# Four places instead of six for first rows, eight instead of six for value rows

## What is computed

```python
def peer_ffn(h, w_q, sub_k1, sub_k2, exp_u, exp_v):       # blocks of 128 tokens
        q1, q2 = jnp.split(split_heads(hb @ w_q, PEER_HEADS), 2, axis=-1)
        ...                                               # top 16 of each half, top 16 of the sums
        idx = jnp.take_along_axis(cand_i, pos, axis=-1)
        gate = jax.nn.softmax(best_s, axis=-1).astype(hb.dtype)
        act = jax.nn.gelu(jnp.einsum('thkd,td->thk', exp_u[idx], hb))
        return jnp.einsum('thk,thkd->td', gate * act, exp_v[idx])
```

## Time and profile before

| | us |
|---|---|
| median of 3 runs | 5725.39 |
| lowest, highest | 5721.04, 5725.57 |
| profiled execution | 5726.25 |
| its span (first to last instruction) | 5724.5 |

### The profile page before, as it was taken

One profiled execution on the slowest core, in us unless ns is written; L12 is line 12 of the kernel. 1 busy time (PEld: TensorE's weight loads), 2 busy tenths in 40 slices (PEclk: granted clock), 3 DMA queues, 4 the chain that ended last, 5 costly groups with the idle time before them and its releaser, 6 DMA issues.

```text
span 5724.5 us, 57220 instructions
## 1 busy us (share of the span) xinstructions
PE 4378.9 (76%) x19168; PEld 2442.8 (43%) x19168; DVE 2919.4 (51%) x7856; ACT 1361.0 (24%) x3807; POOL 2761.2 (48%) x2566
## 2 busy tenths in 40 slices
PE   7988888887987878987855557898777889855555
PEld 4467643433675334653411114567443456511111
DVE  1212756775126767456565541322666654666653
ACT  1411123443212331121211112631143311111111
POOL 0000556666205555666576771000566556677776
PEclk9789888888998889998867768999888899976677
DMA  5543889988638878999998994123888799999999
GB/s 187 194 165 135 318 336 346 335 323 306 216 131 306 293 274 326 390 369 349 349 364 321 370 360 146 41 92 133 315 326 305 273 347 409 363 364 368 347 366 333
DMA packets 464705, 1659.07 MB, mean 290 GB/s; under 512 B 51232, under 2 KB 57504, under 8 KB 464160
## 3 DMA queue, kind: packets, MB, share of 16 engines
q0 software_dynamic: 368640, 1342.34, 63.0%
q1 hardware_dynamic: 95776, 313.07, 15.0%
HBM read 1649.44 MB, written 5.77 MB: 289 GB/s over the span
## 4 chain that ended last, share of the span: by engine, by line
PE 40%; POOL 18%; DVE 13%; issue 11%; DMA 8%; another core or an unknown queue 4%; ACT 4%; PEld 1%; SPq 0%; PEldq 0%; DVEq 0%; POOLq 0%; ACTq 0%
PE banks L669 14%; POOL ub L1474 9%; POOL vb L1485 9%; PE banks L952 8%; DMA vb<-in_peer_v_dram,idx 5%; DVE ub L1425 5%; PE banks L758 3%; PE banks L685 3%; PE banks L860 2%; PE banks L837 2%; PE banks L848 1%; PE banks L798 1%; PE banks L924 1%; DMA wring<-w_gate_dram 1%
## 5 line engine op out<-in xcount | busy, mean ns | idle before, releaser
L1474 POOL DMA_INDIRECT ub<-in_peer_u_dram,idx x1280 | 1411.5, 1103 | 2198.7 <-DVE idx L1413 1293.2
L952 PE MATMUL banks<-vb,dg 128*64 128x512 f32 x5120 | 1588.9, 748 | 685.1 <-DMA vb<-in_peer_v_dram,idx 539.7
L1425 DVE CUSTOM_DVE_ANT_0 ub<-ub,h2cur 128x1024 f32<-128x1024 f32 x1280 | 1527.9, 1221 | 663.5 <-DMA ub<-in_peer_u_dram,idx 426.2
L1485 POOL DMA_INDIRECT vb<-in_peer_v_dram,idx x1280 | 1349.2, 1054 | 747.1 <-issue 349.1
L952 PEld LDWEIGHTS banks<-vb,dg 128*64 128x64 f32 x5120 | 411.7, 162 | 1594.5 <-issue 1474.5
L669 PE MATMUL banks<-region,wring 128*128 128x256 f32 x3840 | 883.4, 389 | 41.5 <-ACT region L1016 25.3
L669 PEld LDWEIGHTS banks<-region,wring 128*128 128x128 f32 x3840 | 736.4, 194 | 224.4 <-issue 115.3
L1172 ACT ACTIVATE dg<-consts,wgt 128x64 f32<-128x64 f32 x1280 | 360.3, 338 | 851.5 <-PE banks L952 314.3
L669 PE MATMUL banks<-h2T,wring 128*128 128x256 f32 x1280 | 309.4, 398 | 26.0 <-ACT h2T L1016 25.0
L837 PE MATMUL banks<-region 64*128 64x256 f32 (+3 forms) x576 | 256.8, 570 | 89.0 <-issue 36.4
L1366 DVE SCALAR_TENSOR_TENSOR region<-region,banks 128x256 f32<-128x256 f32 x120 | 50.5, 421 | 512.2 <-PE banks L669 433.7
(11 more groups left out here) (147 smaller groups left out, 3841.1 us busy)
## 6 DMA issues: line engine op xcount, KB each, us to landing
wring<-w_gate_dram SPq DMA_DIRECT2D x120, 512.0 KB
wring<-w_mod_dram SPq DMA_DIRECT2D x96, 512.0 KB
wring<-w_pq_dram SPq DMA_DIRECT2D x80, 512.0 KB
wring<-w_branch_dram SPq DMA_DIRECT2D x60, 512.0 KB
wring<-w_out_dram SPq DMA_DIRECT2D x40, 512.0 KB
ub<-in_peer_u_dram,idx POOLq DMA_INDIRECT x1280
vb<-in_peer_v_dram,idx POOLq DMA_INDIRECT x1280
region<-in_na_rpb_dram SPq DMA_DIRECT2D x64, 256.0 KB
```

Source lines behind the costliest of these rows:

```text
L952: ins = nc.tensor.matmul(bank(ACC[a])[64 * g:64 * g + 64, :], dg[:, n % DG_RING, :], vb[:, n % V_RING, a * 512:(a + 1) * 512], start=first ...
L1425: nc.vector.tensor_tensor_reduce(out=ub[:, n % U_RING, :], in0=ub[:, n % U_RING, :], in1=h2cur[:, g, :], scale=1.0, scalar=0.0, op0=ALU.mu ...
L1474: pool.indirect_dma_start(ub[:, n % U_RING, :], None, u_rows, bass.IndirectOffsetOnAxis(ap=idx[:, u % IDX_RING, j:j + 1], axis=0)).then_in ...
L1485: pool.indirect_dma_start(vb[:, n % V_RING, :], None, v_rows, bass.IndirectOffsetOnAxis(ap=idx[:, u % IDX_RING, j:j + 1], axis=0)).then_in ...
```

## The change

The ring of first rows gets four places and that of value rows eight. Both rings have places of the same size, so the memory used stays the same. With the new numbers, the first gather of pair p waits for the first dot product of pair p - 2, and the value rows of pair p wait for the sum of pair p - 4.

```diff
 W_SLOTS, W_LEN = 4, 1024
-U_RING, V_RING, IDX_RING, DG_RING = 6, 6, 22, 8
+U_RING, V_RING, IDX_RING, DG_RING = 4, 8, 22, 8
 DIAG_LEAD, SUM_LAG = 2, 11
```

## The result

The changed kernel takes 5881.24 us (median of 3 runs, 5874.3 to 5900.84) against 5725.39: 1.0271 times as long, with a 95% interval of 1.0245 to 1.0298. That is 156 us more; 150 were forecast. The profiled execution took 5881.24 us, its span 5879.4 us. Against the earlier trace rows, DVE, ACT and POOL are busy for 1 to 15 us more, and PE for 71 us more with the same number of instructions; its idle time grew by 84 us, from 1346 to 1429.

What follows compares the result with a forecast made beforehand. PE and its short waits were taken to bound foreground and merging stages, gather traffic the background; 45 + 86 + 29 - 10 = 150 on 5725.4 gave 5875 us, range 5737 to 6030 (5760 to 5990 at 0.60).

Steps and rivals of the forecast that it cites:

- The lead is the shorter ring's: POOL's single queue: the smaller ring leads both gather kinds, so the lead falls from three pairs to two.
- Item 1: Merging stages, 89 pairs: value rows land late, 45 us, a third of the upper end of 134 us.
- Item 2: Other foreground, 329 pairs: one pair in seven waits 1.8 us on PE, 86 us; upper end 250 us.
- item 5: Whole kernel: nothing else changes, same instructions in the same order, engines waiting for the same events; no us added.
- Item 3: Background, 222 pairs: 5 interruptions of DVE, each losing four gathers' advance, 5.8 us; 29 us, ends 0 and 58.
- 10 to 20 us each: Foretold lengthening of each of the two background stretches, with a DMA share a little below 0.94 and 0.97.
- Item 4: After the last dot product, twice in the program: eight value places help, at most 6 us each time; -10 us taken.
- The fit of 3.2 us for a gather: Landing time by a skill's rule, 2.0 us plus bytes at 436 GB/s; two pairs would be enough except at interruptions.
- two pairs are enough: Rival for the whole kernel: a 14 us average spacing covers a 10.5 us way, no change, 5725 us; chance 0.09.
- the value ring holds POOL: Rival: POOL's 259.7 us of waits for sums delay both gather kinds; eight places give -52, 5674 us; chance 0.07.
- Every foreground pair pays: Rival: late landings delay DVE and then PE; upper ends, 432 us more, 6157 us; over 5990 us has chance 0.14.
- The last sign of being wrong: PE's foreground wait for value rows grows but stretches don't get longer, so waits only change names; no size given.

Runs made afterwards that it cites:

- e5: The change itself (four first-row places, eight value-row places) run again on another chip, against the kernel before: 5829.55 us, ratio 1.0242.
- e6: Kernel before with four first-row and six value-row places instead of six and six, on the chip of e5: 5812.79 us, ratio 1.0230.
- e2: Kernel before, rings six and six, POOL's first-row wait two pairs back only in the foreground outside the merging stages: 5547.45 us, ratio 1.0241.
- e4: Kernel before, rings six and six, POOL's first-row wait two pairs back only in the background stretches: 5440.85 us, ratio 1.0070.
- e1: Kernel before with four first-row and six value-row places instead of six and six, on the faster chip: 5621.87 us, ratio 1.0384.
- e8: Changed kernel (four and eight), POOL issuing value rows of pair p - 10 ahead of first rows of pair p; against kernel before: 5709.13 us, ratio 1.0032.
- e11: Kernel before with six first-row and four value-row places instead of six and six: 5820.01 us, ratio 1.0227.
- e12: Kernel before with eight first-row and four value-row places instead of six and six: 5830.04 us, ratio 1.0237.
- e3: Kernel before, rings six and six, POOL's first-row wait two pairs back only in the merging stages: 5456.20 us, ratio 1.0074.
- e10: Kernel before, rings six and six, POOL issuing value rows of pair p - 10 ahead of first rows of pair p: 5889.69 us, ratio 1.0355.

## Why the prediction was right, point by point

- **The lead is the shorter ring's.** Shown for the change: on one chip 4 and 8 and 4 and 6 cost the same (1.0242 and 1.0230, e5 and e6), the shorter lead alone on rings of six and six costs as much as the shorter ring (e2 to e4 against e1), and another order of the line takes most of the loss away (e8). 6 and 4 and 8 and 4 give 1.0227 and 1.0237 (e11, e12), with other parts behind the same total.
- **Item 1, merging stages, 45 us.** The traces give 36, e3 gives 45. The reason named for taking a third of the upper end, quicker landings with fewer gathers queued, is in the trace: 10.4 to 7.5 us. But the prediction told the long landings by the DMA share of 0.96 and more, and its short one of 5.73 us lies in the stretch with 0.97; in the background, at 0.93 to 0.97, the median is 5.8 and 5.9 us. The DMA share isn't what makes a landing long. What the merging stages have besides is the traffic of the weights (before the change the gathers take 76% and 78% of the DMA engines' time there, and 94% and 96% in the background, all that is busy); that it is the reason wasn't tested.
- **Item 2, other foreground, 86 us.** The traces give 88, and that it came so close is luck. The price was of waits alone (one pair in seven at 1.8 us), and item 5 has nothing else change. But 45 of the 88 us are PE doing the same instructions at a lower granted clock, and only 43 are idle time of PE. PE's waits for value rows grew there by 100 us, of which more than half took the place of other idle time; with the merging stages they are 51 places more, and 2.4 us each instead of 1.8. The spacing was also taken too short: a pair comes every 2593 / 329 = 7.9 us there, so two pairs are 16 us and not 14, and even so they weren't enough. On the faster chip e2 measured 136.
- **Item 3, background, 29 us.** The traces give 32, e4 gives 30. The total was right, its working wasn't: not 5 interruptions at 5.8 us but 19 places, over which 32 us are 1.7 each on average. That a pair less in advance is partly made up afterwards would explain it and wasn't tested. "10 to 20 us each" was wrong too: 4 in the first stretch and its gap, 28 in the second, and only the latter moved its DMA share (0.97 to 0.94).
- **Item 4, the end, -10 us.** About -3 at the very end and -4 at the end of layer 0, where 5 were taken for each. The working has a miscount: the earlier trace rows spans ten pairs, so the spacing before was 3.2 us and not 3.6, and the 2.9 to 3.3 foretold for after would have been met without any change. In the traces of one chip the last sum comes 37.4 us (end) and 36.9 us (layer 0) after the last dot product with eight value places (e5), and 38.7 and 41.2 us with six (e6); in whole runs the gain doesn't show.
- **The fit of 3.2 us for a gather**, which the prediction takes from the Trainium skill, "DMA: Bandwidth & Descriptors", section "Anatomy of one DMA — SWDGE (gpsimd) path". By it the rival "two pairs are enough" would have come true. The trace doesn't agree: even the program's first gather, with no other ahead of it, has a landing event 4.4 us after its issue began (566.16 to 570.58 us), and the medians in the stream are 5.8 us and more. It was right to go by the rows: e2 to e4 show that two pairs are not enough in any kind of stretch.
- **What was foretold of the profile.** POOL's wait for dot products well up and in nearly twice as many places, that for sums down to 63 us, PE's foreground wait for value rows at 227 us (150 to 250 foretold): all there.
- **The rivals.** "Two pairs are enough" and "the value ring holds POOL" are excluded by the result. "Every foreground pair pays" took the upper ends, at which all pairs of the merging stages and a third of the others pay their full shortfall. The foreground's waits on landings grew by 144 us on PE and 90 on DVE for 124 us of time, far from its 384. The last sign of being wrong, that PE's waits only change their names, came half true: 144 us of waits for value rows made 74 us of idle time.

## What to carry to other kernels

Where two rings are filled from one in-order queue, count the lead of both in steps of the plan: each is at most that of the shorter ring while both kinds are in the line, so moving places from one to the other shortens both, and added places behind a shorter ring buy nothing until one kind has run out. Ask whose wait is dear: here 229 us less on PE against 224 us more on DVE was a gain of 105 in the same stretches, so if a ring must be short, issue first what the engine on the critical path needs, as long as the other isn't starved (e10). Compare the way from release to use (release, issues of all that stands in between, landing) with the spacing of steps, and expect a loss well before the averages meet, because steps are not evenly spaced. And look at the busy time of the engine that is made to wait, not at its waits alone: here 71 of the 155 us by which the span grew are PE taking longer for the same instructions.

## What the runs showed of the hardware that was not expected

- The kernel before took 5411 us on one chip, and 5725, 5690 and 5695 in the other three sets of runs. In a background stretch the gathers came in at 383 GB/s and a DMA share of 0.99 there (e3), against 351 GB/s and 0.94 on the first chip. Its mean granted clock was higher too, 0.864 to 0.876 in the runs of the kernel before against 0.839 to 0.856 on the other two chips with such runs. The loss by four and six places was 1.0384 on the faster chip and 1.0230 on a slower one: a ratio of two kernels need not carry over between chips.
- With a third fewer gathers in advance, the median landing in the merging stages fell from 10.4 to 7.5 us, while the stages moved 351 and 367 GB/s instead of 372 and 388. On the faster chip it was 11.3 and 11.6 us with six places ahead (e2, e4) and 8.0 with four (e1, e3). In the background, at as high a DMA share, it was 5.8 to 5.9 us with six and with four places on the first chip.
- How often the sums ran at half the granted clock follows how long PE stood for value rows: 1345 records of L952 with 293 us of such waits (e8), 1605 with 715 (e5) and 1625 with 765 (e6) on one chip. That the standing lowers the clock fits this and wasn't tested by itself.
